# State space: waves on ScalarE a turn ahead, cosine from the half angle, double buffers, and raw weight pieces counted by SyncE

## The reference, cut to what matters

```python
lam_bar = jnp.exp(lam * dt)                       # complex, one for each group and state
b_bar = ((lam_bar - 1.0) / lam)[..., None] * b
bu = jnp.einsum("blgh,gph->blgp", uf, b_bar)
states = associative_scan(s -> lam_bar * s + bu)  # over the tokens
y = jnp.real(jnp.einsum("blgp,ghp->blgh", states, c)) + d * uf
```

## Time and profile before

| | |
|---|---|
| median of 3 runs | 4785.81 us (4785.29 to 4788.25) |
| profiled execution | 4786.56 us |
| its span | 4784.9 us |
| TensorE busy (matmul) | 4072.6 us, 85% |
| VectorE busy | 2645.0 us, 55% |
| ScalarE busy | 1595.9 us, 33% |
| GpSimd busy | 24.2 us, 1% |
| mean granted TensorE clock | 0.916 |

### The profile page before, as it was taken

The page is one execution under the profiler, slowest core; times in us unless marked ns, Lnnn a source line. Parts: engine busy times, 40 slices in busy tenths (PEclk is TensorE's granted clock), DMA queues, the critical chain, the costliest instruction groups (busy, mean ns, idle before and its releaser), DMA issues. The chain is left out here.

```text
span 4784.9 us, 67612 instructions
## 1 busy us (share of the span) xinstructions
PE 4072.6 (85%) x24872; PEld 3592.6 (75%) x24872; DVE 2645.0 (55%) x3959; ACT 1595.9 (33%) x2019; POOL 24.2 (1%) x45
## 2 busy tenths in 40 slices
PE   7876669998569999999999989965947779998679
PEld 7863369986358888888888879954946769997559
DVE  4578855446876556556556555425464654543444
ACT  4211034341134444444444434313311113432333
POOL 0000000000000000000000000000000000000000
PEclk9988889998899999999999999966978889998779
DMA  6322235342246566566566545500520005453104
GB/s 213 118 97 92 75 115 163 124 167 88 100 181 207 185 203 206 185 207 206 184 207 204 185 145 181 174 22 19 184 79 0 0 0 176 168 183 120 45 24 161
DMA packets 181901, 645.54 MB, mean 135 GB/s; under 512 B 24744, under 2 KB 27048, under 8 KB 179888
## 3 DMA queue, kind: packets, MB, share of 16 engines
q1 hardware_dynamic: 173040, 619.51, 38.9%
q0 software_dynamic: 2304, 20.97, 1.2%
q10 hardware_dynamic: 6336, 1.84, 0.2%
HBM read 621.26 MB, written 20.99 MB: 134 GB/s over the span
## 5 line engine op out<-in xcount | busy, mean ns | idle before, releaser
L1738 DVE TENSOR_TENSOR weights_trailing<-weight_ring,weights_leading 128x1024 fp32r<-128x1024 f32 x512 | 624.2, 1225 | 567.5 <-ACT weights_leading L1702 566.7
L382 DVE TENSOR_TENSOR weights_trailing<-weight_ring,weights_leading 128x1024 fp32r<-128x1024 f32 x504 | 613.3, 1225 | 549.2 <-ACT weights_leading L377 548.8
L377 ACT ACTIVATE weights_leading<-weight_ring 128x1024 fp32r<-128x1024 f32 x504 | 531.3, 1058 | 747.1 <-PE lin_in_acc L476 332.3
L1702 ACT ACTIVATE weights_leading<-weight_ring 128x1024 fp32r<-128x1024 f32 x512 | 539.3, 1060 | 689.5 <-PE dense_down L1692 352.1
L1670 PE MATMUL dense_up<-pe_parts,weights_leading 128*128 128x512 f32 x2048 | 722.5, 400 | 30.5 <-DVE weights_trailing L1738 16.7
L1692 PE MATMUL dense_down<-weights_leading,dense_act_parts 128*128 128x512 f32 x2048 | 630.4, 389 | 0.0
L1670 PE MATMUL dense_up<-pe_parts,weights_trailing 128*128 128x256 f32 x2048 | 554.0, 281 | 0.0
L476 PE MATMUL lin_in_acc<-lin_in_parts,weights_leading 128*128 128x256 f32 x2432 | 445.2, 286 | 31.1 <-DVE weights_trailing L382 31.1
L1670 PEld LDWEIGHTS dense_up<-pe_parts,weights_leading 128*128 128x128 f32 x2048 | 379.1, 188 | 116.9 <-issue 21.2
L1692 PEld LDWEIGHTS dense_down<-weights_leading,dense_act_parts 128*128 128x128 f32 x2048 | 384.4, 188 | 79.4
L476 PEld LDWEIGHTS lin_in_acc<-lin_in_parts,weights_leading 128*128 128x128 f32 x2432 | 383.5, 193 | 32.1 <-issue 31.2
(11 more groups left out here) (580 smaller groups left out, 6087.0 us busy)
## 6 DMA issues: line engine op xcount, KB each, us to landing
weight_ring<-in_w_experts SPq DMA_DIRECT2D x512, 512.0 KB, 4.2
weight_ring<-in_w_in SPq DMA_DIRECT2D x216, 512.0 KB, 3.4
weight_ring<-in_w_out SPq DMA_DIRECT2D x112, 512.0 KB, 4.2
weight_ring<-in_w_att SPq DMA_DIRECT2D x64, 512.0 KB, 4.3
weight_ring<-in_w_key SPq DMA_DIRECT2D x32, 512.0 KB, 3.5
weight_ring<-in_w_value SPq DMA_DIRECT2D x32, 512.0 KB, 3.5
weight_ring<-in_w_query SPq DMA_DIRECT2D x32, 512.0 KB, 3.7
weight_ring<-in_w_o SPq DMA_DIRECT2D x32, 512.0 KB, 3.8
```

What stands on the lines that cost most here:

```text
L377: self.nc.scalar.activation(leading, x, ACT.Copy).then_inc(self.led, 1)
L382: return self.nc.vector.tensor_tensor(trailing, x, leading.bitcast(F32), ALU.subtract)
L1702: nc.scalar.activation(ring.leading[:, b], ring.ring[:, b], ACT.Copy).then_inc(split_led, 1)
L1738: v.tensor_tensor(ring.trailing[:, b], ring.ring[:, b], ring.leading[:, b].bitcast(F32), ALU.subtract).then_inc(ring.split, 1)
```

## The change

- ScalarE rounds the phase itself (`whole`) and makes sine and cosine (`wave`) for turn i + 1 before it takes up turn i's evict. The cosine comes from the half angle: 1 - 2 sin^2, as a sine, a square and an affine pass. The sine and cosine buffers are doubled. The phase on VectorE is four operations of 128x256 in place of seven passes of 128x1024.
- GpSimd mixes C in seven operations into one of two buffers, and loads `b_in`, which has two buffers; the first two loads go through SyncE.
- TensorE drives turn i + 1 in the middle of turn i's values.
- VectorE adds d x u for turn i - 1 after the first six operations of turn i. The scans read the decay broadcast. The loops over turns are written out.
- The leading and trailing slots of the weight ring belong to the stages that split, and their memory is free in others (`split_slots`).
- SyncE waits for `freed` itself and counts `split` in the raw stages (`rest_raw`); ScalarE waits only before it evicts.

```diff
+    def rest_raw(self, sp, job):
+        _, _, tiles, per = self.jobs[job]
+        for c in range(self.SLOTS, tiles * per):
+            sp.wait_ge(self.freed, self.first[job] + c - self.SLOTS + 1)
+            sp.sem_inc(self.split, 1)
+            self.load(sp, job, c)
+        for c in range(self.SLOTS):
+            sp.wait_ge(self.freed, self.first[job + 1] + c - self.SLOTS + 1)
+            sp.sem_inc(self.split, 1)
+            self.load(sp, job + 1, c)
     def landings(self, n, per, at):
...
         for c in pieces:
-            act.wait_ge(self.ring.freed, self.position(n, c)[0] + 1)
-            act.sem_inc(self.ring.split, 1)
             if c == self.per - 1:
+                act.wait_ge(self.ring.freed, self.position(n, c)[0] + 1)
                 if self.tokens:
                     out = self.dst[:, :, bass.ds(n * WIDE, WIDE) if not isinstance(n, int) else slice(n * WIDE, (n + 1) * WIDE)]
...
                 sp.dma_start(c_src[:], a["ssm_c"]).then_inc(c_here, 16)
+                for i in range(2):
+                    sp.dma_start(b_in[:, i], a["ssm_b"][i * P:(i + 1) * P]).then_inc(b_first[i], 16)
                 values.on_sync(sp)
...
             def _(pool):
...
+                tt = nc.gpsimd.tensor_tensor
+                gi = 2 * GROUP_IN
+                pool.wait_ge(c_here, 16)
+                pool.wait_ge(ready, 1)
+                for i in range(turns):
+                    if i >= 2:
+                        pool.wait_ge(driven, i - 1)
+                        pool.dma_start(b_in[:, i % 2], a["ssm_b"][i * P:(i + 1) * P]).then_inc(b_here[i % 2], 16)
+                        pool.wait_ge(observed, i - 1)
+                    here = lambda n: c[n][:, i * quad:(i + 1) * quad].unsqueeze(2).to_broadcast([P, quad, gi])
+                    cr, ci = c_src[:, i * quad:(i + 1) * quad, 0], c_src[:, i * quad:(i + 1) * quad, 1]
+                    use, part = c_use[:, i % 2], c_tmp[:, i % 2]
+                    tt(part, cr, here("fr"), ALU.mult).then_inc(mixed, 1)
+                    tt(use[:, :, 2], ci, here("fi"), ALU.mult).then_inc(mixed, 1)
+                    pool.wait_ge(mixed, i * 7 + 2)
+                    tt(use[:, :, 0], part, use[:, :, 2], ALU.subtract).then_inc(mixed, 1)
+                    tt(use[:, :, 1], use[:, :, 2], part, ALU.subtract).then_inc(mixed, 1)
+                    pool.wait_ge(mixed, i * 7 + 4)
+                    tt(part, cr, here("nfi"), ALU.mult).then_inc(mixed, 1)
+                    tt(use[:, :, 2], ci, here("nfr"), ALU.mult).then_inc(mixed, 1)
+                    pool.wait_ge(mixed, i * 7 + 6)
+                    tt(use[:, :, 2], part, use[:, :, 2], ALU.add).then_inc(mixed, 1)
...
+                def whole(i):
+                    if i > 0:
+                        act.wait_ge(phased, i)
+                    for q in range(quad):
+                        at = i * quad + q
+                        ins = nc.scalar.activation(rnd[:, q], k.const("time"), ACT.Identity, bias=k.const("round"),
+                                                   scale=c["turn"][:, at:at + 1])
+                    ins.then_inc(rounded, 1)
+                    act.wait_ge(rounded, i + 1)
+                    nc.scalar.activation(rnd[:], rnd[:], ACT.Identity, bias=back[:]).then_inc(wholed, 1)
+                def wave(i):
+                    b = i % 2
+                    act.wait_ge(phased, i + 1)
+                    if i >= 2:
+                        act.wait_ge(observed, i - 1)
+                    nc.scalar.activation(sn[:, b], ang[:], ACT.Sin, scale=TWO_PI).then_inc(waves, 1)
+                    nc.scalar.activation(cs[:, b], ang[:], ACT.Sin, scale=TWO_PI / 2).then_inc(half_waved, 1)
+                    act.wait_ge(half_waved, i + 1)
+                    nc.scalar.activation(cs[:, b], cs[:, b], ACT.Square, scale=float(np.sqrt(2.0))).then_inc(squared, 1)
+                    act.wait_ge(squared, i + 1)
+                    nc.scalar.activation(cs[:, b], cs[:, b], ACT.Identity, bias=k.const("ones")[:, 0:1], scale=-1.0).then_inc(waved, 1)
+                whole(0)
+                wave(0)
                 act.sem_inc(values.beside_taken, 1)
...
+                for i in range(turns):
+                    if i + 1 < turns:
+                        whole(i + 1)
+                        wave(i + 1)
+                    values.on_scalar(act, i // 2, part_of_tile[i % 2])
...
-                    pe.wait_ge(b_here, i * 16 + 16)
+                def drive(i):
+                    pe.wait_ge(b_here[i % 2] if i >= 2 else b_first[i], max(1, i // 2) * 16)
+                    if i > 0:
+                        pe.wait_ge(bu_taken, i)
                     for q in range(quad):
                         for part, bu in enumerate((bu_r, bu_i)):
-                            mm = nc.tensor.matmul(bu[:, q], b_in[:, q, part], u[:, bass.ds(i, 1)].rearrange("p a t -> p (a t)"),
-                                                  start=True, stop=True)
+                            mm = nc.tensor.matmul(bu[:, q], b_in[:, i % 2, q, part], u[:, i], start=True, stop=True)
                     mm.then_inc(driven, 1)
-                    values.on_tensor(pe, n, part_of_tile[m])
+                def observe(i):
+                    b = i % 2
+                    pe.wait_ge(mixed, i * 7 + 7)
                     pe.wait_ge(rotated, i + 1)
-                    for n, (part, prod) in enumerate(((0, p0), (1, p1), (2, p2), (2, p3))):
+                    if i > 0:
+                        pe.wait_ge(taken, i)
+                    for n, (part, prod) in enumerate(((0, wr), (1, wi), (2, cs[:, b]), (2, sn[:, b]))):
                         for q in range(quad):
                             rows = slice(32 * q, 32 * q + 32)
-                            mm = nc.tensor.matmul(y[rows, 0:SEQ], c_use[:, q, part], prod[:, q],
+                            mm = nc.tensor.matmul(y[rows, 0:SEQ], c_use[:, b, q, part], prod[:, q],
                                                   start=n == 0, stop=n == 3, skip_group_check=True)
                     mm.then_inc(observed, 1)
-                    pe.wait_ge(taken, i + 1)
-                with pe.Fori(0, values.tiles) as n:
-                    for m in range(2):
-                        turn(n * 2 + m, n, m)
+                drive(0)
+                for i in range(turns):
+                    pieces = list(part_of_tile[i % 2])
+                    values.on_tensor(pe, i // 2, pieces[:2])
+                    if i + 1 < turns:
+                        drive(i + 1)
+                    values.on_tensor(pe, i // 2, pieces[2:])
+                    observe(i)
...
+                def phase(i):
+                    dve.wait_ge(wholed, i + 1)
+                    for q in range(quad):
+                        at = i * quad + q
+                        ins = v.scalar_tensor_tensor(out=ang[:, q], in0=time, scalar=c["turn"][:, at:at + 1], in1=rnd[:, q],
+                                                     op0=ALU.mult, op1=ALU.subtract)
+                    ins.then_inc(phased, 1)
+                phase(0)
...
+                ch.then(v.tensor_scalar(c["nfr"][:], c["fr"][:], -1.0, None, ALU.mult))
+                ch.then(v.tensor_scalar(c["nfi"][:], c["fi"][:], -1.0, None, ALU.mult))
+                dve.sem_inc(ready, 1)
+                def take(i):
+                    dve.wait_ge(observed, i + 1)
+                    v.scalar_tensor_tensor(out=out[:, i], in0=u[:, i], scalar=k.col("ssm_d")[:, i:i + 1], in1=y[:, 0:SEQ],
+                                           op0=ALU.mult, op1=ALU.add).then_inc(taken, 1)
+                for i in range(turns):
+                    b = i % 2
                     dve.wait_ge(driven, i + 1)
...
+                    dve.wait_ge(waved, i + 1)
+                    dve.wait_ge(waves, i + 1)
+                    if i > 0:
+                        dve.wait_ge(observed, i)
+                    ch.then(tt(wr[:], cs[:, b], bu_r[:], ALU.mult))
+                    ch.then(tt(tmp[:], sn[:, b], bu_i[:], ALU.mult))
                     ch.then(tt(wr[:], wr[:], tmp[:], ALU.add))
...
+                    ch.then(tt(wi[:], cs[:, b], bu_i[:], ALU.mult))
+                    ch.then(tt(tmp[:], sn[:, b], bu_r[:], ALU.mult))
+                    dve.sem_inc(bu_taken, 1)
                     ch.then(tt(wi[:], wi[:], tmp[:], ALU.subtract))
...
+                    if i > 0:
+                        take(i - 1)
+                    if i + 1 < turns:
+                        phase(i + 1)
                     for q in range(quad):
...
+                        decay = c["decay"][:, i * quad + q:i * quad + q + 1].to_broadcast([P, SEQ])
+                        v.tensor_tensor_scan(zr[:, q], decay, wr[:, q], 0.0, ALU.mult, ALU.add)
+                        ins = v.tensor_tensor_scan(zi[:, q], decay, wi[:, q], 0.0, ALU.mult, ALU.add)
                     ch.then(ins)
...
+                    tt(wr[:], cs[:, b], zr[:], ALU.mult)
```

(52 more changed lines are left out.)

59 lines of the change are left out of this document (6 added, 53 removed).

## The result

The kernel after takes 4705.01 us, the median of four runs (4702.32 to 4709.84), beside 4787.03 us for the kernel before (median of four, 4785.29 to 4792.31). The ratio is 0.9824, with a 95% interval from 0.9811 to 0.9836. On the median shown ahead of the prediction that is 4701.6 us (4695.4 to 4707.3), 84 us less, where 67.8 us less was forecast. The profiled execution took 4704.41 us, 82.15 us less than the profiled one of before.

The account below looks back on a forecast made before the run. VectorE was taken to bound the state-space stage; turns of 22.95 instead of 31.57 us gain 65.1 us there, plus 2.7 in the expert choice, 67.8 in all: 4718 us, 8-in-10 range 4704 to 4736.

Parts of the forecast that it names:

- VectorE's work: State-space turn: products, last turn's addition, new phase, scans and four products, 19.15 us without contention.
- The last turn: State-space turn 7, with no phase and no mixing: 20.75 us, ending at 555.9.
- the cover that was claimed: State-space turn: ScalarE's wave starts when the phase ends and is needed 13 us later, so its time is covered.
- The first product: Start of the state-space stage: first product at 374.5 instead of 378.19.
- the wait for the observing: End of a state-space turn: VectorE waits for TensorE's sixteen small matmuls, 3.2 us, ends 2.3 and 4.04.
- the contention: State-space turn: GpSimd's mixing slows VectorE by 0.6 us a turn, ends 0 and 3.5; 1.0 in turn 0.
- The expert choice: First head: VectorE's 4.06 us wait goes, the second head's score is next; 2.7 us gained, between 0 and 4.06.
- TensorE didn't become the bound: State-space rival: TensorE bounds at 22.99 us a turn plus 1.3 of gaps, 24.3; total 4727.5; chance 10%.
- GpSimd didn't stop VectorE: State-space rival: GpSimd stops VectorE for all of its 3.5 us a turn; total 4738; chance 8%.
- nothing went to the low clock for whole turns: State-space rival: TensorE at 1.2 GHz for whole turns, 38.1 us each, 48 us lost; total 4834; chance 3%.
- The one for a clock that is up and no contention: State-space rival: 11.4 us more gained, 4706.6; low end of the main case, no chance of its own.
- The change doesn't do what it says: State-space rival: VectorE still waits for the waves each turn; total 4786; chance 1%.

Follow-up runs that it names:

- the kernel with three mixings: Changed kernel with GpSimd's seven mixing operations done three times a turn, same values: 4726.3 us, a turn of 24.03.
- the kernel without the lead: Changed kernel in which ScalarE makes turn i's waves only once turn i - 1 has been observed: 4738.53 us, a turn of 26.4 us.
- that part alone: At the expert choice: kernel before with only rest_raw, SyncE waiting for freed raw pieces and counting split: ratio 0.9988 [0.9978, 0.9998].

## Why the prediction was off, step by step

**What held.** The direction, the bound and the new wait. VectorE's work was forecast at 19.15 us a turn without contention (18.71 in the first) and measured at 19.17 in the mean of seven after (21.74 − 2.57); with the wait gone a turn takes 19.17. The scans from the broadcast decay take 0.67, as from a copy. The last turn took 20.72 (545.32 − 524.60) against 20.75, and there the wait was 3.11, near the 3.2 of the forecast. ScalarE's waves have the cover that was claimed: they are ready at 386.29 for a start at 394.19, and taking the lead away costs 4.7 us a turn. The first product came at 372.44 instead of 374.5, 1.8 of it drift from before the stage.

**The failed step in the stage: the wait for the observing, 3.2 us.** The prediction put it "in the middle" between 2.3 at the high clock and 4.04 at the low. It measured 2.57: all observings began at 2.4 GHz, the clock stayed up through four of the seven and fell amid the other three. This is 0.63 a turn. The middle was a choice between two ends, not a reading: the row behind it has 3.87 us of idleness in another stage, TensorE idled 0.94 to 2.07 here, and the 2.5 us that the forecast gave it don't follow from its own turn (22.95 − 19.05 is 3.9; only the gaps of 1.3 us named in a rival bring it near 2.5).

**With it the contention, 0.6 us, 1.0 in the first turn.** It measured 0.3 in the first turn (21.75 − 2.75 is 19.00 against 18.71) and 0.04 in each of the others. In the later turns one GpSimd operation of seven meets VectorE's third product, and it is GpSimd's that waits. The timeline of both, kernel after:

```profile
418.10 1.22 DVE L1032 TENSOR_TENSOR ssm_wr<-ssm_wr,ssm_tmp 128x1024 f32<-128x1024 f32 x1
418.16 1.47 POOL L950 TENSOR_TENSOR ssm_c_use<-ssm_c_tmp,ssm_c_use 128x128 f32<-128x128 f32 x1
```

GpSimd's takes 1.47 instead of 0.46, VectorE's 1.22 as ever. Only in turn 0, with fourteen operations, is VectorE slowed: 1.31 and 1.35. Both times a GpSimd operation was already under way when VectorE's began, as in the kernel with three mixings; at 418.10 VectorE's had begun first. The row that the term came from, 1.05 against 0.76, is a pair of short operations beside copies, and doesn't scale to this. The rule in "SBUF — State Buffer", "Who interferes with whom", of the Trainium skill named the right operations: those with two SBUF inputs are met, those that read PSUM are not. The size that I gave it, 0.5 to 1.0 us a turn, was too high: the loss fell on GpSimd. The two terms are 8.4 us too much in seven turns, 4.4 for the wait and 4.0 for the contention; with 0.2 at the start and roundings that is the stage's 8.8 (73.9 − 65.1).

**The expert choice.** 2.7 was forecast, 3.9 measured after and 3.1 with that part alone: the score came earlier too.

**What was missing.** The forecast had no term for the dense experts, and this is the step that takes the time out of its range: with the stage's 8.8 and the expert choice's 1.2 put right, 4718.0 becomes 4708.0, which is inside. Written-out instructions ahead of the dense experts took 8.1 us from that stage without touching it, and 6.2 us [1.4 to 11] from the whole by the ratio; 4708.0 less 6.2 is 4701.8, and 4701.6 was measured. The three parts add up: 73.9 in the stage, 6.2 for the written-out loop, 3.1 to 3.9 for the expert choice are 83.2 to 84.0; 84 was measured. That they meet so closely is partly luck, since the 6.2 has an interval of 5 us to either side and other stages moved by as much.

**What stays open.** The 10.6 us given back behind the dense experts. Against the first profile of before, the same stretch took between 8.0 us less and 10.5 more in the other eleven executions, 5.6 more on average, and 3.3 more in the unchanged kernel. So a good part may be that the first profile of before was quick there; the rest wasn't taken apart. And of the issue waits it is shown that they are few once a loop ahead in TensorE's program is written out, not by what mechanism.

The rivals: TensorE didn't become the bound (it idles 0.94 to 2.07 us for VectorE's last product in a turn, and with half of the values' matmuls left out the turn got longer), GpSimd didn't stop VectorE, nothing went to the low clock for whole turns. The one for a clock that is up and no contention, 4706.6, is what the stage did in four turns of seven. "The change doesn't do what it says" fell with the kernel without the lead.

## What to carry to other kernels

Where an engine's turn ends in a wait for another's small work, price that wait at both clocks and look how long the other engine idles before it; here, moving the mixing off the waiting engine gave nothing, and a second buffer gave the whole wait. Price contention by the operations that meet, one by one, and say which of the two engines is the one that waits. And when a change writes out code on TensorE, other stages can move too (0.13% of the whole here); try that part alone before crediting it to the design.

## What the runs showed of the hardware

- TensorE began its small matmuls at 2.4 GHz after an idleness of 2.07 us in a turn of 21.4 (its groups 0.43 us apart) and fell to 1.2 GHz amid them in three cases of five. With half of the values' work it began at 1.2 GHz after 3.10 us (0.85 apart), though at 2.4 once after 4.06.
- At the head of a loop's pass TensorE stood up to 2.7 us with nothing to wait for in the profile. The sum over one stage was 6.5 to 13.8 us with a loop ahead of it in TensorE's program, and 0.7 to 2.6 with that loop written out.
- A GpSimd tensor_tensor of 128x128 takes 0.39 to 0.46 us, VectorE's 0.28. When GpSimd's meets a VectorE operation with two SBUF inputs that is under way it waits for most of its 1.22 us (1.32 to 1.48 instead of 0.39 to 0.46). VectorE's loses 0.09 to 0.13 us when GpSimd's was under way first. Beside many of GpSimd's in a row VectorE's scans take a fifth to a third longer, and GpSimd's own up to 0.84.
- ScalarE changes between copy, square, sine and cosine by half angle here in consecutive passes of 1.02 to 1.15 us over 128x1024, without a load of tables between them; one such load took 1.28 us.
